# One hand-written order of pieces for all engines becomes one order per engine, in two mixers, two cross attentions and two blocks

## The reference, cut to what matters

```python
for layer in range(2):                                  # first network
    x = x + 0.5 * swiglu(rms_norm(x), ...)              # stages f0, f2
    h = rms_norm(x, mix_norm[layer])
    x = x + (diff_stickbreak_mixer(h) if layer == 0     # stage m0
             else mla_mixer(h))                         # stage m1
    x = x + memory_cross_attention(rms_norm(x), mem)    # stages c0, c1
    x = x + 0.5 * swiglu(rms_norm(x), ...)              # stages f1, f3
for l in range(2):                                      # second network
    mix = concat([gla(x), rwkv7(x), nsa(x)]) @ w_out[l] # stages b0, b1
    x = layer_norm(ALPHA * x + mix)
    x = layer_norm(ALPHA * x + (silu(x @ w_gate) * (x @ w_up)) @ w_down)   # f4, f5
```

## Time and profile before

| | |
|---|---|
| median of the three runs | 2066.3 us |
| profiled execution, its own time | 2062.06 us |
| its span in the trace | 2060.3 us |
| around the span | 1.8 us |
| TensorE busy / VectorE / ScalarE / GpSimd | 96% / 73% / 54% / 19% |
| mean granted TensorE clock | 0.984 |

### The profile page before, as it was taken

One profiled execution on the slowest core, in us unless ns is written; L12 is line 12 of the kernel. 1 busy time (PEld: TensorE's weight loads), 2 busy tenths in 40 slices (PEclk: granted clock), 3 DMA queues, 4 the chain that ended last, 5 costly groups with the idle time before them and its releaser, 6 DMA issues.

```text
span 2060.3 us, 32937 instructions
## 1 busy us (share of the span) xinstructions
PE 1967.7 (96%) x12514; PEld 1716.7 (83%) x12514; DVE 1506.8 (73%) x2676; ACT 1114.4 (54%) x2045; POOL 386.3 (19%) x347
## 2 busy tenths in 40 slices
PE   8999999999999999899999998899999999899998
PEld 6888888888888888798888977688888887688887
DVE  7976876787678767777876688578766688577765
ACT  5654566565455546655654543456555543456554
POOL 3521002222112210022220011101222012111212
PEclk9999999999999999999999998899999999999999
DMA  7555433355555555144655440235555340234552
GB/s 264 192 177 200 158 133 124 122 185 180 180 193 194 177 194 172 43 154 150 193 178 195 141 141 5 77 98 173 194 180 189 101 137 14 78 113 158 188 177 93
DMA packets 88719, 309.84 MB, mean 150 GB/s; under 512 B 9840, under 2 KB 11632, under 8 KB 88176
## 3 DMA queue, kind: packets, MB, share of 16 engines
q1 hardware_dynamic: 88272, 305.03, 44.4%
q10 hardware_dynamic: 288, 2.69, 0.4%
HBM read 306.63 MB, written 1.05 MB: 149 GB/s over the span
## 4 chain that ended last, share of the span: by engine, by line
PE 80%; DVE 11%; ACT 4%; issue 2%; POOL 1%; DMA 1%; SPq 0%; DVEq 0%; ACTq 0%; POOLq 0%
PE ps L134 79%; DVE scratch L159 3%; ACT scratch L148 2%; DVE w_lo L159 2%; PE ps L139 2%; DVE stats L176 1%; DVE scratch L165 1%; POOL rows L159 1%; DVE scratch L186 1%; ACT w_hi L148 1%; ACT L153 1%; DVE x L159 1%; DMA ring<-in_w 0%; DVE scratch L171 0%; DVE stats L159 0%
## 5 line engine op out<-in xcount | busy, mean ns | idle before, releaser
L134 PE MATMUL ps<-h,w_hi 128*128 128x512 f32 (+1 forms) x2912 | 893.2, 367 | 20.3 <-DVE w_lo L159 15.8
L159 DVE TENSOR_TENSOR w_lo<-ring,w_hi 128x1024 fp32r<-128x1024 f32 (+3 forms) x573 | 696.7, 1227 | 295.1 <-ACT w_hi L148 291.4
L148 ACT ACTIVATE w_hi<-ring 128x1024 fp32r<-128x1024 f32 (+3 forms) x573 | 584.8, 1030 | 410.1 <-PE ps L134 406.4
L134 PE MATMUL ps<-h,w_lo 128*128 128x256 f32 x2512 | 706.3, 281 | 0.0
L134 PEld LDWEIGHTS ps<-h,w_hi 128*128 128x128 f32 x2912 | 524.4, 190 | 118.9 <-issue 15.5
L134 PEld LDWEIGHTS ps<-h,w_lo 128*128 128x128 f32 x2512 | 477.9, 190 | 0.0
L134 PE MATMUL ps<-f,w_hi 128*128 128x512 f32 (+1 forms) x1444 | 417.1, 355 | 0.1
L134 PE MATMUL ps<-f,w_lo 128*128 128x256 f32 x1184 | 331.3, 280 | 0.0
L159 POOL TENSOR_TENSOR f<-f_work,f 128x256 fp32r<-128x256 f32 x132 | 185.9, 1409 | 572.4 <-ACT f L148 572.3
L134 PEld LDWEIGHTS ps<-f,w_hi 128*128 128x128 f32 x1444 | 254.3, 189 | 41.2 <-issue 0.4
L134 PEld LDWEIGHTS ps<-f,w_lo 128*128 128x128 f32 x1184 | 223.9, 189 | 0.1
(11 more groups left out here) (157 smaller groups left out, 2020.3 us busy)
## 6 DMA issues: line engine op xcount, KB each, us to landing
ring<-in_w SPq DMA_DIRECT2D x518, 512.0 KB, 4.2
ring<-in_w SPq DMA_DIRECT2D x48, 384.0 KB, 3.6
ring<-in_w SPq DMA_DIRECT2D x16, 396.0 KB, 3.1
ring<-in_w SPq DMA_DIRECT2D x8, 256.0 KB, 4.6
stage_consts<-in_ctwo ACTq DMA_DIRECT2D x1, 1346.0 KB, 6.8
stage_consts<-in_cthree ACTq DMA_DIRECT2D x1, 1283.0 KB, 5.7
x<-in_x SPq DMA_DIRECT2D x4, 256.0 KB, 6.2
scratch<-in_m SPq DMA_DIRECT2D x1, 1024.0 KB, 11.2
```

What stands on the lines that cost most here:

```text
L134: return self.e.matmul(out, lhsT, rhs, start=start, stop=stop, skip_group_check=free)
L148: return self.e.activation(out, x, func, **k)
L159: return self.e.tensor_tensor(out, a, b, op)
```

## The change

Each of the six strings becomes four, one per engine (TensorE, ScalarE, VectorE, GpSimd). Each of them has the same pieces, and each chain keeps its order, but between chains the engines may differ. `order` and `woven` take the engine's name. The splits of these stages are now all placed by marks: the automatic split after a piece is left to the feed-forward stages, and one at the end of each woven stage remains. The split's assertion that the unit four before belongs to an earlier piece is gone.

The marks in the strings (after: `z` only for TensorE, `.` only for ScalarE, `,` only for VectorE; before, those in the strings, the rest being automatic):

| stage | z before, after | . before, after | , before, after |
|---|---|---|---|
| m0 | 7, 0 | 27, 40 | 29, 38 |
| c0 | 8, 8 | 6, 6 | 7, 9 |
| m1 | 9, 3 | 26, 33 | 24, 31 |
| c1 | 8, 8 | 7, 7 | 9, 9 |
| b0 | 32, 5 | 28, 37 | 32, 38 |
| b1 | 76, 8 | 27, 37 | 30, 37 |

In c0 and c1 every engine's own pieces stand in the order they had. The diff, with b0 and c0 alone of the strings:

```diff
+ENGINES = ("pe", "act", "dve", "pool")
 MARKS = {"z": "warm", ".": "split_hi", ",": "split_lo"}
 WEAVE = {
-    "b0": ("zr,.r,z..,r.,.,r.r,..rgk,,kth..g..rg,.rkr,.rhk,,rhg,hl.,t,tht,.,hrhl,h,,.h.h,hrrlrrhhrhzhhzrhzhr"
-           "hsrhsshsshrsnrsnnrrnznznrrznrrsursvrszusrursrvsurunsvnrrnrvvrnrzzuurvrvnr.uvuvruvuzrzv,,.rm.zm,z"
-           ".,znzzuvzzmmmm,mm.m...,,m,mmmm.mmmmmmmm.mmmmmm,mzzzzzzzzzzzzmmmmm,,mmmmm"),
-    "c0": ("pp.p,,.pzpzz.zzpbdcazbda.c,,bacdooo.zooooo,,.oo,oz"),
+    "b0": (
+        "rrrrrrkkgrthggghhrrkklmttthhsslsshhhsrhhhrrrlrrrrhhsrhrsrhhhrshrhrshhhsnnnsrrnrznnnuvrrvvursrrurusrnrsvv"
+        "nzrrruurnruvrvrnuurvrvrnumrvvunvummmmmmmmmmmmmmmmmmmmmmmmmmmzzmzmmmmmmmmm",
+        "..rr...rr.k..rr..s.kkgs..hg.r.tgrghhh..rrrkrrrr..sttlth.h..shhhhl...shhhhlhrrsrrrshhsrrsrhhhhshssrrrnnnn"
+        "nnnuvrrvvruuursrrrnvvrnrrrrrrunuvuur.unrrvvrvnruuvvvmmm....mmmm.ummmmm.mm..mmm.mmmmsmmmm.mmmmmmmm.mmmmmm"
+        "n",
+        ",,,,rr,krr,,rr,r,rrk,,k,th,,r,khhh,,r,ttls,,,hh,shsslhts,,,rrhghrrhlrrhhsrhrhsrhrhhrshrshnrhsnnhnnnnsrru"
+        "vuvrrvrsggrrurnsvvurrsnrurrrunruvrgvurvunuvuvrrrv,rmmm,unvm,mmmm,,,,m,,mmmmmmmmmmmmmmmmmmm,,mmmmmmm,mmmm"
+        ",n",
+        "hvvssrrrrrhgnhhhhhhrgvhhrrrvrhhhhhrmssshullsskvvrrrrvhhvkggvkrrrrrtrrrhrvuurvnrhhmsssmmmsrrmmslsuuumrrrm"
+        "knnnnnnrrrunurrnhmsmrrmmmmmmmmrrrmmtttuummmmmvummmmmmnmrrrrmmmmmnn",
+    ),
+    "c0": (
+        "ppppzpzzzzpbdcazbdacbacdozooooozooooo",
+        "..pppp.ppbdcabda.cbacdooo.ooooo.ooo",
+        ",,,,ppppppbdcabdac,,bacdoooooooo,,oo,o",
+        "ooooooooooppppppbbbdddcccaaao",
+    ),
...
 }
@@ def act_split(e, K):
     if u.pair >= NU:
-        before = K.pairs[u.pair - NU]
-        assert before.piece <= e.piece, (u.n, u.piece, e.piece)
-        e.wait_ge(*K.used(before))
+        e.wait_ge(*K.used(K.pairs[u.pair - NU]))
...
-def woven(stage, chains):
-
+def woven(stage, chains, engine):
+
+    word = WEAVE[stage][ENGINES.index(engine)]
     for mark, piece in MARKS.items():
-        chains[mark] = [(piece, i) for i in range(WEAVE.get(stage, "").count(mark))]
+        chains[mark] = [(piece, i) for i in range(word.count(mark))]
     its = {k: iter(c) for k, c in chains.items()}
-    return [next(its[k]) for k in WEAVE.get(stage) or evenly(chains)]
+    out = [next(its[k]) for k in word]
+    assert all(next(it, None) is None for it in its.values()), (stage, engine)
+    return out
...
@@ def act_program(e, K):
-    for name, T, order in stages(K):
-        early = name == "f0" or ("split_hi", 0) not in order
+    for name, T, order in stages(K, e.name):
         for what, i in order:
             if what == "split_hi":
                 act_split(e, K)
             elif what not in MARKS.values():
                 e.piece += 1
                 ACTE[T.kind](e, K, T, what, i)
-                act_splits(e, K, early and (name, what) != ("f0", "x"))
+                if name not in WEAVE:
+                    act_splits(e, K, (name, what) != ("f0", "x"))
+        if name in WEAVE:
+            act_splits(e, K, False)
```

More of the change, by code:

```diff
@@ L49 @@
-    "c0": ("pp.p,,.pzpzz.zzpbdcazbda.c,,bacdooo.zooooo,,.oo,oz"),
[L50 to L54, removed]
+    "b0": (
[8 more added lines that the diff above has]
+        "hvvssrrrrrhgnhhhhhhrgvhhrrrvrhhhhhrmssshullsskvvrrrrvhhvkggvkrrrrrtrrrhrvuurvnrhhmsssmmmsrrmmslsuuumrrrm"
+        "knnnnnnrrrunurrnhmsmrrmmmmmmmmrrrmmtttuummmummvmummmmmmnmrrrrmmmmmnn",
+    ),
@@ new lines @@
+    "c0": (
[3 more added lines that the diff above has]
+        "ooooooooooppppppbbbdddcccaaao",
+    ),
+    "c1": (
+        "pppppzzzzzpdcabzzczadbabcdooooooooooo",
+        "...ppppppdcab.cadbabcd.ooooo.oooo.oo",
+        ",,,,,ppppppdcabcadbabcd,oo,ooo,oooooo,",
+        "ooooooooooppppppdddcccaaabbbo",
+    ),
+    "m0": (
+        "qplqpkkbbbqqqytyyqtsyykksbacykbbcaacvvtcaccaassctsyytcacaatscoooooooooooooa",
+        "qpbbyy...qpk..q....k....qt...klyytq....sbyyks..b..a..bcc.b.aca..vv.qctacacasstcksotcaoocaatacyys......oo"
+        "oo..oooooo.",
+        "p,qq,,,,,yyk,,,,kq,,bbbqqq,t,,l,k,yyk,,s,yyb,,atck,a,,csacc,bb,,vvt,caaoypccassatcy,a,caooacttss,,,,,,oo"
+        "oooo,oooo",
+        "cqkkbbbpaqccoosoyyykooaotyytbtoskaqtqcyvyvqloacyccsastooaaaaoossqpocccatbbk",
+    ),
@@ L55 @@
+    "m1": (
+        "qqpqkqqkkqquyyyuqqkkuuuuuyytttzkbukctayytdtttzzcbdabbdcdacybdacbdcaoaoooooooqqhhooooo",
+        ".y.qq...q.k.qq.q..qq.kk..yy.u..qqkkq..uu..uuh.uuyypy..tttkkbhcttadttcbdabbddccabdacbyca.d.a....oooo..ooo"
+        "oooo.o.yuto",
+        ",y,qq,,p,qk,qq,,qq,,q,kk,,uu,,yy,qqqkk,,,uuuu,h,yyttybkkcuutthacdbttttdab,dbcbacddcaabc,,yyda,,,,,ooooo,"
+        "oooo,oooo",
+        "ooooooooooooqqqqqqqqqqqyyyyyyyykkkkkkkpuuuuuuuuhhttttttttbbbbbbaaaaaaddddddcccccco",
+    ),
 }
@@ L940, in __init__, with order @@
             self.wg, self.wu, self.wd = (lambda I, n=n: I["ffn_w_" + n][l, h] for n in ("gate", "up", "down"))
-    def order(self):
+    def order(self, engine):
         hi, lo = [("split_hi", 0)] * 2, [("split_lo", 0)] * 2
@@ L1566, in chains, with order @@
                 "o": [("out", 0)] + x_order(range(4)) + [("out", 1)] + x_order(range(4, 9))}
-    def order(self):
-        return woven(self.stage, self.chains())
+    def order(self, engine):
+        return woven(self.stage, self.chains(), engine)
     def head(self, h):
@@ L3531, with stages @@
 POOL = {"ffn": pool_ffn, "mixer0": pool_mixer0, "cross": pool_cross, "mla": pool_mla, "block": pool_block}
-def stages(K):
+def stages(K, engine):
     for name in STAGES:
         T = TABLES[name if name[0] == "m" else name[0]](K, name)
-        yield name, T, T.order()
+        yield name, T, T.order(engine)
 def pe_warm(e, K):
@@ L3574, in dve_program @@
     e.wait_ge(K.S.sem("loaded_c"), 16)
-    for name, T, order in stages(K):
-        early = name == "f0" or ("split_lo", 0) not in order
+    for name, T, order in stages(K, e.name):
         for what, i in order:
@@ L3583, in dve_program @@
                 last = name == "f4" and (what, i) in (("down", (7, 2)), ("x", 7))
-                dve_splits(e, K, early and not last and (name, what) != ("f0", "x"))
+                if name not in WEAVE:
+                    dve_splits(e, K, not last and (name, what) != ("f0", "x"))
+        if name in WEAVE:
+            dve_splits(e, K, False)
 def pool_program(e, K):
     e.wait_ge(K.S.sem("loaded_c"), 16)
-    for name, T, order in stages(K):
+    for name, T, order in stages(K, e.name):
         for what, i in order:
```

18 lines of the change are left out of this document (11 added, 7 removed).

## The result

The change made the kernel faster: 2001.29 us median of 4 executions (1990.42 to 2002.03) against 2064.24 us (2055.45 to 2067.44) for the kernel before, a ratio of 0.9677, 95% interval 0.9647 to 0.9708. That is 63 us, where the forecast had 28. The profiled execution of after is its fastest, 1990.42 us with a span of 1988.6, 11 us under the median. Its b0 of 229 us is no exception: of experiment 8's kernels, the first, with b0 untouched, and the last have 229 us too, the second, also with b0 untouched, 232. What differs is the rest: in the trace of the first (2004.0 us) the feed-forward stages, whose code is the same, are together 12 us longer than in this one.

What follows compares the result with a forecast made beforehand. It took b0 and b1 as held in turn by TensorE and VectorE, and the feed-forward stages as covered by TensorE. The terms summed to -28.1 us: 2062.1 - 28.1 = 2034 us, range of 8 in 10 2004 to 2082.

Steps and rivals of the forecast that it cites:

- The signs named for the order: No w_lo wait at second projections, none before rbon0; four stages' idle near 35 us; b0, b1 245 to 257 us.
- the ceiling: In m0, m1, b0, b1 TensorE idles 62.4 us; a better order can win some 60 us, no more.
- Clock: In the four stages, waits left open where unread products ran bring TensorE to 1.2 GHz: +10 us, bounds +0 to +29.
- Unread products: In the four stages, 108 marks removed free TensorE time, mostly in waits: -5 us, bounds 0 and -20.8.
- Second projection: In b0 and b1, TensorE's waits of 2.7 and 2.9 us for w_lo go whole: -5.6 us.
- rbon0: In b0, TensorE's 3.2 us wait before this piece goes, plus 1.7 us for the clock: -4.9 us.
- The other waits of b0 and b1: Half of TensorE's remaining 20.9 and 18.9 us of short waits there go: -10.4 and -9.4 us.
- m1, m0: Half of TensorE's 9.5 and 4.3 us idle in these stages goes: -4.7 and -2.1 us.
- Splits by hand: In the woven stages, hand-placed weight splits may hold their engine too early: +5 us, between 0 and 11.2.
- Table loads: In b1, ScalarE's table loads fall from ten to seven: -1 us, between 0 and -3.8.
- Stages at nothing: The feed-forward stages, c0 and c1 keep their order or pieces' places: no change in time.
- Most waits go: Rival: in the four stages three quarters of idle and product time vanish, clock costs only 2: 2002 us, chance 0.13.

Runs made afterwards that it cites:

- experiment 8: After with b1's nq0 and nqT0 earlier: 2000.40 us; that plus m1's nine unread products: 2001.32 us; after plus 72 unread marks at remaining waits: 1997.19 us.
- experiment 1: Kernel before with 108 unread-product marks taken out: 2081.58 us, ratio 1.0068; kernel after with before's numbers of products: 2005.97 us, 0.9703.
- experiment 4: Kernel after, but TensorE takes gd0 and gl0 of b0 behind rbon0 again: 2006.96 us, ratio 0.9725.
- experiment 5: Kernel after, but VectorE takes nq0 and the two nqT of b0 behind gO2: 2008.13 us, ratio 0.9715.
- experiment 3: Kernel before with rp2's splits ahead of rp0 in b0 and b1: 2057.43 us; kernel after with the leading splits behind rp0 again: 2009.71 us.
- experiments 1, 2 and 4: The 2 here: kernel before with 64 more unread-product marks in b0, ahead of the eight longest-waiting pieces: 2059.50 us, ratio 0.9954.

## Why the forecast was wrong, step by step

The signs named for the order came true: no wait for w_lo at the second projection, none to speak of before rbon0, idle time in the four stages "near 35 us" (34.5), under 60 `ps<-consts` instructions (40). b0 and b1 were to be 245 to 257 us long and are 229 and 239; they lost 62 us together, beyond the 45 that the text named as its own refutation.

*The step that failed* is the ceiling: "an order that overlaps them better has some 60 us of waits to draw on, no more". Only idle time was counted as what an order can win. With its products unchanged the order alone won 61 us (experiment 1), while the idle time in the four stages fell by only about 30. Some 24 us more were booked as busy, above all real products run at half rate behind waits; the unread products that stood in waits are the other busy time that was not work. A forecast with half of the idle time and nothing else in it reproduces the idle time that was found and misses half of the gain.

*Clock*, +10: the wrong sign. The step was reasoned as products removed from a schedule that keeps its waits. For that schedule the sign was right and the size low: -108 marks in the old order cost 14.5 us, where this term and the next say +5 together, and the real products of b0 and b1 took 15.2 us more. In the new order the longest waits were gone, the clock of b0 went from 0.94 to 1.00, and 19 us of busy time were won (39.1 less the 19.7 that unread products filled). Only in m1 did it come as forecast, 0.99 to 0.96, at some 2 us. The step took the waits as it found them and the gain from the order as a separate sum; the one depends on the other.

*Unread products*, -5 of 20.8: near for the new order, where taking them out won about 5 us (experiment 1; not sure by the ratios, while b0 and b1 alone are 15 shorter in the traces), and nothing in the old one. They filled 19.7 us less of TensorE's time; the rest of that are waits that they hid, which the order removed.

*Second projection*, -5.6: right in place, low in size. Alone in the old kernel it gave 9.6 us (interval 5 to 14), taken back in the new one it cost 8 to 12. *rbon0*, -4.9: the wait went as said. Whether the two pieces moved ahead of it did that or VectorE's own order is not shown: experiment 4 leaves gt0 uncovered, as neither order does, and the stall there cost 10 us of b0.

*The other waits of b0 and b1*, -10.4 and -9.4, and *m1, m0*, -4.7 and -2.1: as idle time, right (b0 and b1 -22.5 of the 28.6 forecast with the two leading waits and rbon0's 3.2, m1 and m0 -5.3 of 6.8); as time, low. "VectorE at 9.6 to 10 of 10 us speaks against all" was a poor brake: VectorE was busy with pieces that TensorE did not wait for, and a piece of its own order at the right time is worth 11 us of b0 (experiment 5). VectorE's saturation says that it has work, not that it has *this* work.

*Splits by hand*, +5: wrong sign; no wait of TensorE on w_lo stands among after's long ones in b0 or b1, and the leading splits are a gain (experiment 3). *Table loads*, -1: b1 has 6 in place of 10, one fewer than said, and no effect of it can be seen. *Stages at nothing*: c0 and c1 are within 1.5 us, the feed-forward stages within 3.5 us of before either way, as they differ between executions.

The case with nearly this number, "Most waits go" at 2002, had 0.13. Its mechanism is right in that the four orders fit and the products vanish, wrong in its idle time: three quarters of the 62.4 were to go, under half did. What speaks for the price of a wait as the runs show it (a stall of 3.95 us costing 10.3, two of 6.7 together costing 11.5, one of 9.1 costing 11.4) is the clock behind it: 5.0, 7.0 and 3.8 us of these are busy time. The Trainium skill (TensorE: Matmul & The Clock Gate, section on HAM oscillation) describes a stall that the array pays for again in slow products after it; experiments 1, 2 and 4 agree, with 14.5, -10 and 10.3 us. The forecast had weighed the clock for the products' removal alone, not for the order.

Open: which engine's own order bears most of the gain. Engines were not exchanged one at a time; that the new order of one would not fit the old orders of the others is argued, not shown. Experiments 4 and 5 show one move each of TensorE and of VectorE.

## What to carry to other kernels

Before taking idle time as the ceiling for a reordering, add what is booked as busy and is not work: filler products, and the part of real products that ran at the low clock (here b0 of before, at 0.94, had 14.8 us of it and b1, at 0.97, 7.5). Price a long wait of TensorE at its length plus the clock behind it (here 10.3 us for one of 3.95, 11.5 for two of 6.7 together, 11.4 for one of 9.1), and treat order and fillers as one question: in b0 and b1 fillers paid while the waits stood and cost once they were gone; in m1, with them, the clock was 1.00, and 0.96 without. When an engine is nearly saturated, ask which of its pieces the waiting engine waits for before calling it the bound.

## What the runs showed of the hardware

64 more unread products, 125 instructions, shortened b0 from 264 to 257 us and the kernel by about 10, the granted clock of the stage going from 0.94 to 0.99. The same seven or eight products (128x256, out of the ring) took 0.58 us each behind a stall of 3.95 us at a clock of 0.52 and 0.31 us each at 1.00. And idle time by itself does not lower the clock: the 10 us of 1260 to 1270 in after have 2.58 us of it in short waits at 1.00, while the earlier trace rows has 2.34 us in 1260 to 1270 at 0.83.
